# Input projection: x turned in 32x32 blocks on VectorE instead of on TensorE, the token scale applied to the results

## What is computed

```
h    = rmsnorm(x, norm1_g)                 # mean of squares over 1024, per token
proj = h @ w_in                            # 1024 -> 512 q | 128 k | 128 v | 512 u
q, k = rope(rmsnorm(q)), rope(rmsnorm(k))  # per head of 64
a    = softmax(q k^T / 8) v                # 8 query heads, 2 key heads
p    = pooled u (windows 2, 4, 8, 16) minus u, 4 group matrices, a scale
x    = x + concat(a, p) @ w_out
x    = x + relu(rmsnorm(x, norm2_g) @ w_up)^2 @ w_down
```

## Time and profile before

| | |
|---|---|
| median of 3 runs | 1500.82 us |
| span of the profiled execution, first to last instruction | 1499.2 us |
| its own time as a run | not given; the median is 1.6 us above the span |
| projection, start to the last tile's results | about 0 to 200 us |
| TensorE busy | 1490.5 us, 99% |
| VectorE, ScalarE, GpSimd busy | 1015.6, 718.0, 394.7 us |
| granted TensorE clock | 1.000 over the span |

### The profile page before, as it was taken

The page is one execution under the profiler, slowest core; times in us unless marked ns, Lnnn a source line. Parts: engine busy times, 40 slices in busy tenths (PEclk is TensorE's granted clock), DMA queues, the critical chain, the costliest instruction groups (busy, mean ns, idle before and its releaser), DMA issues.

```text
span 1499.2 us, 23419 instructions
## 1 busy us (share of the span) xinstructions
PE 1490.5 (99%) x8031; PEld 1328.7 (89%) x8031; DVE 1015.6 (68%) x1287; ACT 718.0 (48%) x1215; POOL 394.7 (26%) x348
## 2 busy tenths in 40 slices
PE   9999999999999999999999999999999999999999
PEld 8999988888878889999999999999888888888887
DVE  7434489999965567445445444548888878878875
ACT  6323289999943335555445455546332323223220
POOL 3356379988940000000000000000411311311300
PEclk9999999999999999999999999999999999999999
DMA  6110021100145737523333432438743443442434
GB/s 237 50 36 18 18 78 29 29 11 11 33 171 182 266 142 305 236 101 143 135 128 112 156 138 101 146 132 314 266 151 119 133 154 104 143 158 94 144 99 182
DMA packets 69113, 195.19 MB, mean 130 GB/s; under 512 B 5560, under 2 KB 7744, under 8 KB 68928
## 3 DMA queue, kind: packets, MB, share of 16 engines
q1 hardware_dynamic: 66992, 183.36, 34.8%
q10 hardware_dynamic: 2064, 11.08, 1.8%
HBM read 119.97 MB, written 67.63 MB: 125 GB/s over the span
## 4 chain that ended last, share of the span: by engine, by line
PE 93%; ACT 2%; POOL 2%; DVE 1%; issue 1%; DMA 0%; SPq 0%; ACTq 0%; POOLq 0%; DVEq 0%
PE ps L794 24%; PE ps L796 23%; PE ps L795 23%; PE ps L1096 6%; PE ps L974 4%; PE ps L1106 3%; PE ps L956 2%; PE ps L958 2%; PE ps L989 2%; PE ps L990 2%; ACT prob L1327 1%; PE ps L1116 1%; PE ps L803 1%; POOL prob L2401 0%; ACT pThi L1232 0%
## 5 line engine op out<-in xcount | busy, mean ns | idle before, releaser
L794 PE MATMUL ps<-h,wuhi 128*128 128x384 f32 (+1 forms) x904 | 301.3, 333 | 0.2 <-issue 0.2
L796 PE MATMUL ps<-h,wulo 128*128 128x384 f32 (+1 forms) x904 | 301.1, 333 | 0.0
L795 PE MATMUL ps<-h,wuhi 128*128 128x384 f32 (+1 forms) x904 | 301.1, 333 | 0.0
L794 PE MATMUL ps<-wdhi,hidhi 128*128 128x512 f32 x672 | 261.5, 389 | 0.1
L796 PE MATMUL ps<-wdhi,hidlo 128*128 128x512 f32 x672 | 261.4, 389 | 0.0
L795 PE MATMUL ps<-wdlo,hidhi 128*128 128x512 f32 x672 | 261.4, 389 | 0.0
L2202 DVE TENSOR_TENSOR yacc<-yacc,ps 128x1024 f32<-128x1024 f32 x167 | 203.3, 1217 | 77.1 <-PE ps L796 77.0
L1232 ACT ACTIVATE hidhi<-hin 128x1024 fp32r<-128x1024 f32 (+1 forms) x72 | 86.9, 1207 | 300.8 <-PE ps L796 291.7
L2116 DVE TENSOR_TENSOR u<-u,ps 128x384 f32<-128x384 f32 x96 | 53.1, 553 | 181.2 <-PE ps L796 181.1
L794 PEld LDWEIGHTS ps<-h,wuhi 128*128 128x128 f32 x904 | 169.7, 188 | 0.6 <-issue 0.4
L795 PEld LDWEIGHTS ps<-h,wuhi 128*128 128x128 f32 x904 | 169.7, 188 | 0.0
(11 more groups left out here) (221 smaller groups left out, 2822.1 us busy)
## 6 DMA issues: line engine op xcount, KB each, us to landing
hd<-hout SPq DMA_DIRECT2D x64, 384.0 KB, 3.2
hin<-hd SPq DMA_DIRECT2D x48, 512.0 KB, 3.7
hd<-hout SPq DMA_DIRECT2D x32, 576.0 KB, 2.8
hin<-hd SPq DMA_DIRECT2D x24, 768.0 KB, 4.3
wuraw<-in_w_up SPq DMA_DIRECT2D x17, 1024.0 KB, 6.0
wdraw<-in_w_down SPq DMA_DIRECT2D x8, 2048.0 KB, 9.5
h<-h2d ACTq DMA_DIRECT2D x7, 1536.0 KB, 10.9
x2in<-in_x SPq DMA_DIRECT2D x12, 512.0 KB, 3.4
```

The costliest lines, as they stand in the source:

```text
L794: pe.matmul(out, w_hi, m_hi, start=start, stop=False, skip_group_check=resumed)
L795: pe.matmul(out, w_hi, m_lo, start=False, stop=False, skip_group_check=resumed)
L796: return pe.matmul(out, w_lo, m_hi, start=False, stop=stop, skip_group_check=resumed)
```

## The change

- x tiles come a second way: four DMAs of 32 partitions each. Quarter q of the partitions gets feature columns 256q to 256q+255, of the four 32-token blocks side by side (pieces of 1 KB). VectorE transposes 32x32 blocks (`turn_x`, one instruction of 128x1024 per tile) straight into `xT` in SBUF. Its input steps 8 elements (32 bytes) from one column to the next. The k-tile then holds features 8p+k, and so w_in's rows and g1 are loaded in that order too.
- TensorE's transposes of x and of g1 go, and `scale_x` goes.
- The squares need rows: each tile is loaded once more as it was (`load_rows`, on SyncE's queue, each waits for the square before it).
- r, kept for all tiles in `rs`, is applied as the scale of ScalarE's copies of q, k and v, and for v's lo part in one `scalar_tensor_tensor` on VectorE. For u it must lie along the free axis: `rs` of a pair goes to DRAM and comes back broadcast (`turn_rs`, two small DMAs per pair on SyncE's queue, with a wait between them), and u is copied out by a VectorE multiply instead of a ScalarE copy.
- `project_qkv` alternates between banks 0, 1 and 2, 3.
- On GpSimd `norm_x(t + 2)` stands behind the head scale of tile t.
- The loops of the projection are written out.

```diff
+            def load_x(t):
+                if t >= 2:
+                    sp.wait_ge(xT_done, t - 1)
+                for q in range(4):
+                    sp.dma_start(quarter_in(t % 2, q), quarter_of(t, q)).then_inc(x_in[t % 2], 16)
+            def load_rows(t):
+                if t:
+                    sp.wait_ge(ssx_done, t)
+                sp.dma_start(stat_area(), x[t * P:(t + 1) * P]...).then_inc(xn_in, 16)
+            def turn_rs(p):
+                sp.wait_ge(rsx_done, 2 * p + 2)
+                sp.dma_start(rsd[p], rs[:, 2 * p:2 * p + 2]).then_inc(rs_out, 16)
+                ...
+                sp.wait_ge(rs_out, 16 * (p + 1))
+                sp.dma_start(rsb[:, p % 2], rsd[p]...partition_broadcast(P)).then_inc(rs_in, 16)
             # SyncE's opening
+            for k in range(3): load_wi(k)
+            load_x(1)
+            for k in range(3, KT): load_wi(k)
+            load_rows(0)
+            load_wi_u(0)
+            load_wi_u(1)
+            load_x(2)
             sp.dma_start(gqkb[:], ...)
+            load_rope(0)
+            load_rows(1)
+            load_x(3)
+            (ident, load_rope(1)), turn_rs(0), load_rows(2)
             # TensorE
-            def transpose_x(t): ...            # 8 pe.transpose, L803
-                    if not (last and i >= 2):
-                        transpose_x(t + 2)
-            warm(7) ... warm(7)
+            warm(11)
             # ScalarE
+                act.wait_ge(rsx_done, t + 1)    # in copy_qkv
+            def first_pair():
+                for k in range(KT // 2): split_wi_u(k)
+                square_x(1)
+                copy_qkv(0, 0)
+                square_qk(0)
+                for k in range(KT // 2, KT): split_wi_u(k)
             # VectorE
+            def turn_x(t):
+                dve.wait_ge(x_in[t % 2], 64 * (t // 2) + 64)
+                dve.wait_ge(hT_hi, t)
+                dve.wait_ge(hT_lo, t)
+                dve.transpose(blocks_out(), blocks_in(t % 2)).then_inc(xT_done, 1)
             def split_hT(t, i):
-                minus(hTlo..., psw[:, 0:D]..., hThi...)
+                minus(hTlo..., xT[:], hThi...)
+            turn_x(2)                          # behind the last split_wi
             def first_pair():
+                for k in range(KT // 2): split_wi_u(k)
+                split_v(0, 1)
+                sum_squares(0)
+                for k in range(KT // 2, KT): split_wi_u(k)
+                scale_qk(0)
+                gain_qk(0)
+                split_v(1, 3)
+                sum_squares(1)
+                split_hT(2, 2)
+                turn_x(3)
+                rotate(0, 0)
+                scale_qk(1)
+                gain_qk(1)
+                split_hT(3, 3)
+                turn_x(4)
+                rotate(1, 1)
+                save_u_columns(0)
```

More of the change, by code:

```diff
@@ L573, in _ @@
[L573 to L578, removed]
+            for t in range(TT):
+                if t + 4 < TT:
+                    load_x(t + 4)
+                if t + 3 < TT:
+                    load_rows(t + 3)
+                if t % 2 and t + 2 < TT:
+                    turn_rs((t + 1) // 2)
+                if t + 2 < TT:
+                    load_rope(t + 2)
@@ L796, in three, with project_qkv @@
                 return pe.matmul(out, w_lo, m_hi, start=False, stop=stop, skip_group_check=resumed)
[L798 to L809, removed]
-                freed = FIRST + t - (isinstance(t, int) and t == TT - 1)
-                pe.wait_ge(qk_copied, freed)
+            def project_qkv(t, i):
+                buf, tok, bank = i // 2, (i % 2) * P, qkv_banks(i)
+                pe.wait_ge(hT_lo, t + 1)
+                pe.wait_ge(qk_copied, FIRST + t - 1)
                 for out, c0, c1 in ((ps[:, bank, :], 0, 512), (ps[:, bank + 1, 0:QKVW - 512], 512, QKVW)):
                     if c0:
-                        pe.wait_ge(v_lo, freed)
+                        pe.wait_ge(v_lo, FIRST + t - 1)
                     for k in range(KT):
@@ L925, in project_block @@
                     t = n * 4 + i
-                    project_qkv(t, i, 0 if last and i == 2 else 2)
-                    if not (last and i >= 2):
-                        transpose_x(t + 2)
+                    project_qkv(t, i)
                     if i % 2:
@@ L1869, in first_pair @@
                 split_hT(3, 3)
+                turn_x(4)
                 rotate(1, 1)
-                scale_x(4, 0)
+                save_u_columns(0)
             def project_block(n, last):
-                for i in range(2 if isinstance(n, int) and n == 0 else 0, 4):
+                for i in range(2 if n == 0 else 0, 4):
                     t = n * 4 + i
-                    split_v(t, 1 if last and i == 2 else 3)
+                    split_v(t, qkv_banks(i) + 1)
                     sum_squares(t)
-                    if not (last and i >= 2):
+                    if t + 2 < TT:
                         split_hT(t + 2, (i + 2) % 4)
-                    if not (last and i >= 1):
-                        scale_x(t + 3, (i + 3) % 2)
+                    if t + 3 < TT:
+                        turn_x(t + 3)
                     if last and i == 1:
@@ L1894, in project_block @@
                     rotate(t, i)
+                    if i % 2 and not (last and i == 3):
+                        save_u_columns(t // 2)
             first_pair()
@@ L2359, in project_block @@
                     t = n * 4 + i
-                    opens = isinstance(n, int) and t < 2
-                    if not (last and i >= 1) and not opens:
-                        norm_x(t + 3)
                     pool.wait_ge(qk_summed, FIRST + t + 1)
```

304 lines of the change are left out of this document (137 added, 167 removed).

## The result

The changed kernel is slower: 1519.36 us, median of four runs (1513.48 to 1519.58), against 1500.82; ratio 1.0112 (of the runs' means), interval 1.0095 to 1.0129. Three of the four runs took 1519, one 1513.48. The forecast was 1496.2 with a range that ended at 1502.5. The profiled execution took 1519.58 with a span of 1517.8 (1499.2 before).

A forecast was written before the change was run, and what follows sets the result against it. The prediction took TensorE to bound the kernel. Transposes -8.0, opening +2.3, steady pairs +0.8 and the step into the attention +0.3 summed to -4.6 us: 1496.2 us against 1500.82, range 1491 to 1502.5.

The forecast's parts named there:

- What bounds the kernel: Whole kernel: TensorE, busy 99% of the span; an instruction taken off it shortens the kernel unless another engine is late.
- The transposes, -8.0: Projection, x tiles 4 to 11: removing TensorE's transposes saves 2.0 us a pair, 8.0 us over four pairs.
- Alternating banks, nothing: Projection: alternating PSUM banks gains nothing, since no matmul waited for a copy.
- The steady pairs, +0.8: Odd tiles' qk chain: `roped` in time in tiles 3 and 9, 0.4 us more waiting each in tiles 5 and 7.
- The lock: Steady pairs: `hTlo`, now with two SBUF operands on VectorE, holds GpSimd up for its 1.1 us.
- The opening, +2.3: First pair: x 2 lands at about 22, the qk chain stalls TensorE 3.5 us, `project_qkv(2)` at 44.3 against 42.02.
- The step into the attention, +0.3: After the projection: VectorE saves u before `inverses` 2 and 3, GpSimd's `normalize` ends some 2.5 us later, costing 0.3.
- Copying with a scale, nothing: ScalarE's copies: copying with a scale instead of without costs nothing.
- D: Rival, opening: quarter loads are slow, x 2 and rows land 4 or 5 us later, +4.5, 1500.7 us; chance 0.10.
- C: Rival: the turn is slow, reading every eighth element; at 4 us per turn, 1519 us; chance 0.12.
- B: Rival: `hTlo` gets ahead of GpSimd in even tiles too; tiles 3, 5, 7, 9 stall, 1500.2 us; chance 0.17.
- A: Rival: the opening is not late, x 2 lands by 20 or the chain has slack; 1492.0 us; chance 0.17.

The follow-up runs named there:

- one_transpose: The kernel before the change with one of the 8 transposes of each x tile from tile 4 on, nothing put in their place; 1501.7 us, ratio 1.0002.
- order2_one_pair: order2 with tiles 2 to 11 of the projection all in PSUM banks 2 and 3, as in the kernel before; 1518.4 us.
- lo_from_psum: The changed kernel with `hTlo` of tiles from 2 on reading a PSUM operand in place of `xT` (wrong values); 1517.0 us.
- dense_turn: The changed kernel with the turn reading 32 neighbouring columns instead of every eighth one (h comes out permuted); 1515.9 us.
- order2: The changed kernel with engine lists reordered: turn of tile t+2 between sums and `scale_qk` of tile t, `hTlo` behind `rotate(t)`, `qkT(0)` saved earlier; 1512.3 us.
- order3: order2 with the opening's queues and lists mended: g1, `ident`, `gqk` on ScalarE's queue, tile 2's rows ahead of `turn_rs(0)`, `norm_x(2)` behind `qsin` of tile 1; 1503.9 us.
- p128x1k: The changed kernel with x loaded as four DMAs of all 128 partitions, 256 columns each, 1 KB pieces (wrong elements turned); 1511.8 us.

## Why the prediction was wrong

- *What bounds the kernel.* That TensorE's time is what counts was right as a sum and wrong as a price: one_transpose took 7.0 us of the predicted 8.0 off it and gained nothing measurable.
- *The transposes, -8.0.* Right, given the second pair of banks (order2_one_pair). From tile 3 to 4, 5 to 6 and 7 to 8 the distance fell by 1.97, 2.00 and 2.03; from tile 1 to 2 by 0.4, the clock taking 1.6.
- *Alternating banks, nothing.* Wrong: 1.24 per pair, which in the sum is inside the 8.0. "No matmul waited for a copy" was true only because the removed transposes stood in that wait.
- *The steady pairs, +0.8.* +2.9: waits came in at tiles 3, 5, 7 and 9 (+0.33, +0.81, +0.82, +0.94). The lock was seen as predicted, but the sum came 0.4 later than I had it and the turn of 2.20 ends just behind `rsqk`; lo_from_psum shows that the turn alone is enough, dense_turn that with a turn of 1.25 a wait of 0.5 to 0.6 stays, near the forecast's 0.7 in tiles 5 and 7, and order2 that there is none in a better list.
- *The opening, +2.3.* **This step failed**: +19.5. By its own numbers: `second_qkv` at 19.7 came at 24.61 (turns of 2.15, x 1 waited for, late first matmul, clock 0.89); `project_u` at 28.15 came at 36.43, `ident`'s wait of 3.3 not having been priced at all though SyncE's queue was part of the change; "x 2 lands at about 22" came at 31.2 (25.7 to 28.1 in four other executions); and `roped` of tile 0, "36.7", came at 52.55. Of these 15.9, 11.3 were there when gain ended (43.06 against 31.8), behind x 2, 9.2 late, and the square of tile 1, 10.6 late (34.57 against 24). Most of the rest is one clause, that `qsin(0)` goes behind `norm_x(2)` "whose rows come after `turn_rs(0)`": I gave it 2.1 us (31.8 to 33.9), and it took 6.9 (43.06 to 49.94). The landing times were the rate of before times the bytes, with nothing for what quarter loads do to the rate and to SyncE's queue. The runs: order3 takes 11.7 us off tile 1 with the lists and queues alone, p128x1k 8.4 with the loads alone.
- *Slips in the working.* The second four `wilo` (27.6 to 30.6) were left out ahead of scale, 0.5; 19.7 + 8.35 is 28.05, not 28.15. That every pass of VectorE is "priced by its columns alone, 1.2 to 1.3 ns each" did not fit its own rows, where `scale_x` takes 0.74 for 1024. And the `wilo` that "passed beside `rsqk` without delay" took 3.09 for four, where the next four, from 27.33, took 2.73: a delay of 0.36 is not excluded, and "the whole instruction is too much here" does not follow. In tile 4, after, `rsqk` begins 1.0 ahead of the end of `hTlo` and takes 2.82 instead of 1.96.
- *The step into the attention, +0.3.* Not seen.
- *Copying with a scale, nothing.* `qk`'s copy went from 0.71 to 0.80; off the path.
- *Rivals.* D had the right mechanism and a price of 4.5; by p128x1k it was 7.5. C had the right sign, but the turn took 2.15 us, not 4. B's condition did not come (in tile 4 `msqk` starts at 104.03, just ahead of `hTlo`, and takes 0.21), yet its sign, waits in all of tiles 3, 5, 7 and 9, did: +2.9. A was wrong.
- *Open.* Behind tile 11 every kernel with the change took 1.7 to 5.0 us longer than the kernel before (1298.8) in its profiled execution, in code that is the same. A wait in the first MLP block, where the DMA engines are 0.94 busy (620 to 630), holds 0.6 to 2.5 of it (1.45 of the changed kernel's 2.6; 0.45 more is a wait for the load of `wolo` at 454.14):
```profile
630.30 0.41 PE L844 MATMUL ps<-h,wuhi 128*128 128x384 f32 x1 [1.45 <-ACT u L1248]
```
Why it comes was not tried. Nor was the clock of the opening separated from the starvation that goes with it.

## What to carry over

Before pricing an instruction taken off the busiest engine, ask what waits it covered: leave it out alone and look for the wait that appears. Follow every new load to the first in-order list that waits for it, and write down what is queued behind that wait; here a norm needed two tiles later stood ahead of a product needed at once. Price a load by its partitions, its pieces and its slowest dimension, and not by its bytes alone: here each of them changed its rate.

## What the hardware showed unexpectedly

- A 32x32-block transpose on VectorE of 128x1024 f32 takes 1.25 us from neighbouring columns and 2.15 from columns 32 bytes apart.
- While loads into 32 partitions at a time ran, all DMA together moved 168 to 246 GB/s with the engines nine tenths busy; with the same bytes over 128 partitions it was 311 to 417 (6 to 12 us); with a slowest dimension of 4, 94 to 109.
- Four such quarter loads in a row held SyncE's issue for 1.9 to 7.2 us (7.15 at 12.32, 4.09 at 22.92), and with it everything behind them.
